# One-hot matrices built after the residual split, and gates applied one expert step earlier, in a two-block transformer kernel

## The reference, cut to what matters

```
g = jax.nn.softmax(best, axis=-1)
u = expert_u[idx]
act = jax.nn.gelu(jnp.einsum('td,thkd->thk', xc, u), approximate=False)
w = (g * act).astype(h.dtype)
return jnp.einsum('thk,thkd->td', w, expert_v[idx])
```

## Time and profile before

| | us |
|---|---|
| median of 3 runs | 1471.93 |
| the 3 runs | 1464.92, 1471.93, 1472.66 |
| the profiled execution, its own time | 1464.92 |
| its span, first to last instruction | 1463.6 |
| PE busy | 1386.9 (95%) |
| DVE busy | 980.6 (67%) |
| ACT busy | 638.5 (44%) |

### The profile page before, as it was taken

The page is one execution under the profiler, slowest core; times in us unless marked ns, Lnnn a source line. Parts: engine busy times, 40 slices in busy tenths (PEclk is TensorE's granted clock), DMA queues, the critical chain, the costliest instruction groups (busy, mean ns, idle before and its releaser), DMA issues.

```text
span 1463.6 us, 22358 instructions
## 1 busy us (share of the span) xinstructions
PE 1386.9 (95%) x9318; PEld 966.8 (66%) x9318; DVE 980.6 (67%) x1555; ACT 638.5 (44%) x851; POOL 153.7 (10%) x138
## 2 busy tenths in 40 slices
PE   6999899899999798959999999999999999999998
PEld 5655798478864355535888889999997444444443
DVE  2433786389984666557658998899997555555555
ACT  2341422166753433444525454544444444444443
POOL 0221523124530000000010300000000000000000
PEclk9999999899999999979999999999999999999999
DMA  6312000285664342233606655555446565565651
GB/s 259 144 60 84 1 2 1 89 298 180 213 225 144 136 180 72 102 115 116 230 30 235 225 182 197 174 173 180 168 170 229 199 204 202 202 244 201 202 202 57
DMA packets 33140, 231.50 MB, mean 158 GB/s; under 512 B 3712, under 2 KB 3984, under 8 KB 6160
## 3 DMA queue, kind: packets, MB, share of 16 engines
q1 hardware_dynamic: 31968, 227.02, 43.9%
q10 hardware_dynamic: 720, 1.73, 0.3%
q0 software_dynamic: 352, 1.32, 0.2%
HBM read 227.96 MB, written 2.10 MB: 157 GB/s over the span
## 4 chain that ended last, share of the span: by engine, by line
PE 87%; DVE 5%; ACT 4%; issue 3%; DMA 0%; POOL 0%; ACTq 0%; DVEq 0%; POOLq 0%
PE bank L583 21%; PE bank L589 21%; PE bank L586 21%; PE bank L606 7%; PE bank L1191 2%; PE bank L674 2%; PE bank L902 2%; PE bank L733 2%; PE bank L1155 1%; DVE arena L1299 1%; PE bank L691 1%; PE bank L873 1%; PE bank L799 1%; ACT arena L2220 1%; PE bank L790 1%
## 5 line engine op out<-in xcount | busy, mean ns | idle before, releaser
L583 PE MATMUL bank<-arena 128*128 128x256 f16 (+3 forms) x600 | 186.7, 313 | 11.1 <-DVE arena L1291 5.8
L586 PE MATMUL bank<-arena 128*128 128x256 f16 (+3 forms) x600 | 186.5, 313 | 0.0
L589 PE MATMUL bank<-arena 128*128 128x256 f16 (+3 forms) x600 | 186.5, 313 | 0.0
L1299 DVE SCALAR_TENSOR_TENSOR arena<-ring,arena 128x2048 f16<-128x2048 f32 (+1 forms) x59 | 133.7, 2273 | 46.2 <-ACT arena L2220 46.0
L2220 ACT ACTIVATE arena<-ring 128x2048 f16<-128x2048 f32 (+1 forms) x59 | 111.0, 1892 | 37.9 <-PE bank L589 37.9
L2041 DVE SCALAR_TENSOR_TENSOR HT<-ring,HT 128x2048 f16<-128x2048 f32 x41 | 93.9, 2290 | 40.9 <-ACT HT L2581 40.7
L2610 ACT CAST cst<-arena 128x512 f16<-128x512 f32 x64 | 39.4, 617 | 174.2 <-PE bank L589 171.2
L2041 DVE SCALAR_TENSOR_TENSOR ring<-ring 128x2048 f16<-128x2048 f32 x42 | 96.1, 2289 | 28.1 <-ACT ring L2581 27.8
L2041 DVE SCALAR_TENSOR_TENSOR X<-ring,X 128x2048 f16<-128x2048 f32 x42 | 96.1, 2289 | 26.1 <-ACT X L2581 26.0
L1191 PE MATMUL bank<-ring,arena 128*128 128x128 f16 x512 | 98.6, 219 | 0.0
L583 PE MATMUL bank<-cst,X 128*128 128x256 f16 x336 | 91.5, 272 | 0.0
(11 more groups left out here) (355 smaller groups left out, 3323.6 us busy)
## 6 DMA issues: line engine op xcount, KB each, us to landing
ring<-in_expert_u SPq DMA_DIRECT2D x64, 1024.0 KB, 4.9
ring<-in_expert_v SPq DMA_DIRECT2D x64, 1024.0 KB, 4.8
ring<-in_w_in_n SPq DMA_DIRECT2D x24, 1024.0 KB, 4.9
ring<-in_w_up_t SPq DMA_DIRECT2D x22, 1024.0 KB, 5.3
ring<-in_w_down_n SPq DMA_DIRECT2D x11, 1024.0 KB, 4.9
ring<-in_w_out_n SPq DMA_DIRECT2D x8, 1024.0 KB, 4.8
ring<-in_w_query_t SPq DMA_DIRECT2D x8, 1024.0 KB, 5.0
ring<-in_w_in_t SPq DMA_DIRECT2D x3, 1024.0 KB, 7.1
```

The costliest lines, as they stand in the source:

```text
L583: pe.matmul(out_, stat[0], mov[0], start=start, stop=False)
L586: pe.matmul(out_, stat[0], mov[1], start=False, stop=False)
L589: return pe.matmul(out_, stat[1], mov[0], start=False, stop=stop)
L1299: nv.scalar_tensor_tensor(out=lo, in0=ld.slot(i), scalar=W_UP, in1=hi, op0=ALU.mult, op1=ALU.subtract).then_inc(s["split_lo"], 1)
```

## The change: what it does

```
-GATES_IN = {LATE + 35 * g // 31: g for g in range(32)}
+GATES_IN = {LATE + 36 * g // 31: g for g in range(32)}
...
     for q in range(WHOLE, 64):
+        expert_lo(q + 2 - WHOLE)
+        for _ in range(SEARCH.get(q, 0)):
+            next(chosen)
         if q == SLOTS_AFTER[1] + 1:
             next(slots_evicted(1))
         if q + 1 in GATES_IN:
             one_hots(GATES_IN[q + 1])
-        expert_lo(q + 2 - WHOLE)
-        for _ in range(SEARCH.get(q, 0)):
-            next(chosen)
-        if q - 1 in GATES_IN:
-            weigh(GATES_IN[q - 1])
-        if q > LATE:
-            weigh_late(q - 1)
-    w_lo(0)
-    w_lo(1)
-    weigh_late(63)
+        if q in GATES_IN:
+            weigh(GATES_IN[q])
+        if q == 63:
+            w_lo(0)
+            w_lo(1)
+        if q >= LATE:
+            weigh_late(q)
...
-        expert_hi(q + 3 - WHOLE)
         if q in GATES_IN:
             keep_gates(GATES_IN[q])
+        expert_hi(q + 3 - WHOLE)
```

## The result

The changed kernel takes 1478.61 us (median of 9 runs, 1477.68 to 1487.11) against 1464.92 (9 runs, 1463.48 to 1472.66; the first three of these are the ones shown above). The medians are 13.7 us apart, 0.93%. The ratio on record, into which 26 runs of the changed kernel went, is 1.0105, with a 95% interval of 1.0084 to 1.0127: slower by about 1%. The prediction was +13.6 us on the profiled execution, and 1485.5 as the median.

The account below looks back on a forecast made before the run. PE alone was taken to bound the stage, each new wait paid in full. Stalls of 14.8 us less 1.2 at the end gave +13.6: 1478.5 us profiled, median 1485.5, range 1474 to 1489.

Parts of the forecast that it names:

- The one-hots behind the residual: Steps 26 to 62: chain of 8.32 us early, 7.84 late, makes PE's gate matmuls wait; 14.8 us of stalls together.
- The two-step rule: Two PE steps last at least 13.05 us early, 12.57 late, so among neighbours with gates every second step stalls.
- The copies ahead of `expert_hi`: ACT's gate copies lengthen the chain to the one-hots by 0.65 us early, 0.17 late; no row shows them there.
- The weighing one step earlier: On DVE, ahead of the residual, ending near 2.2 us early, 2.9 late: costs nothing early, about nothing late.
- The end of the stage: PE's start of the second stage loses 0.61 us instead of 1.80, a gain of 1.2 us.
- The table: PE's work stays the same; a fifth step without gates adds one dearer stall, already included; expert_v's later load costs nothing.
- The sum and the median: Whole kernel: +13.6 us, profiled execution 1478.5 us, median 1485.5 us.
- the choice of level: Forecast median set at 1471.93 + 13.6, the level where two of the three runs shown stood.
- A: Rival: one-hots come in time for the gate matmuls, only the end's 1.2 us gain remains; 1470.7 us, chance 0.09.
- B: Rival: early chain 0.5 us shorter, neighbours' stalls nearly go, six large ones remain; +5 us, 1477, chance 0.07.
- C: Rival: stalls make PE's clock fall, 3.4 us each; six falls give 1506 us, two 1492; chance 0.08.
- D: Rival: DVE is the bound throughout; expected to bind in the last third alone, so counted within the forecast.

Follow-up runs that it names:

- e1: The changed kernel with the one-hots first again, ahead of the residual; ratio 0.9996 to the kernel before, stage -1.0 us.
- e2: The kernel before with only the one-hots moved behind the residual; ratio 1.0054, stage +8.1 us.
- e5: The kernel before with the one-hots behind the residual and the gate copies ahead of expert_hi; ratio 1.0118, stage +13.9 us.
- e6: The kernel before with only the gate copies moved ahead of expert_hi; ratio 1.0008, stage 0.0 us.
- e7: The changed kernel with the gate copies behind expert_hi again; ratio 1.0296 to the kernel before, stage +40.9 us.
- e10: The changed kernel with the one-hots ahead of the residual and the copies behind expert_hi again; ratio 1.004 to the kernel before, stage +5.0 us.
- e9: The kernel before with the new table alone, groups spread to step 62; ratio 1.0019, stage +1.4 us.
- e4: The changed kernel with PE's gate matmuls begun after the first expert matmul of a step instead of 13; ratio 1.0258 to the kernel before, stage +37.7 us.
- the first four experiments: The runs e1 to e4, beside which runs of the kernel before were taken.
- e8: The changed kernel with the one-hots first again and w_lo(0), w_lo(1) ahead of the last residual; ratio 0.9973 to the kernel before, stage -1.8 us.
- e3: The changed kernel with PE's gate matmuls begun after 25 expert matmuls instead of 13; ratio 0.9989 to the kernel before, stage +0.2 us.

## Why the prediction was right

**The one-hots behind the residual.** Right in mechanism and size. The chain measured 8.28 us against 8.32. By groups of steps the losses were 3.5, 2.7, 2.5, 2.4, 2.9 and 1.3 us (26 to 32, 34 to 38, 41 to 45, 48 to 53, 55 to 60, 62) against 3.6, 2.8, 2.5, 2.2, 2.55 and 1.18: 15.4 in all against 14.8. That the place of the one-hots is the cause is shown from both sides: restored alone, the loss is gone (e1), made alone, it is 8.1 us (e2), and with the copies 13.9 (e5).

**The two-step rule.** Right for the first three groups. In the last two it was only nearly so. The losses there are 1.27, 0.33, 0.40, 0.43, 0.46 us in steps 55 and 57 to 60, step after step and not every second one: DVE's pass of 6.56 us is the bound there, as the prediction had it for steps 55 to 60 with +0.6 us (its own numbers give 0.5). It began one group earlier, from step 51 (0.19, 0.22, 0.25), where DVE after already has nothing idle and a pass is longer than PE's 6.15:

```profile
1057.48 1.05 DVE L2067 SCALAR_TENSOR_TENSOR arena<-bank,arena 128x400 f32<-128x400 f32 x2
1063.84 1.07 DVE L2067 SCALAR_TENSOR_TENSOR arena<-bank,arena 128x408 f32<-128x408 f32 x2
```

That is 6.36 us, 0.21 over PE's step. The prediction looked at the longest passes alone.

**The copies ahead of `expert_hi`.** The unknown of the sum, taken as 0.65 us, was 0.61. Their cost of about 6 us exists only together with the late one-hots (e5, e6).

**The weighing one step earlier.** Costs nothing where the one-hots lead (e1), and nothing early. Late it was to cost "about nothing", and that is 0.2 us at the stage's last residual. That it depends on the copies being first was not in the prediction; e7 and e10 show it.

**The end of the stage.** Forecast 0.61 us lost instead of 1.80; measured 0.77 by the starts (0.60 of recorded idle). The 0.16 more is the weighing ahead of the last residual. The gain is 1.0 us (e1), not 1.2.

**The table.** Taken by itself, it costs 1.4 us at the end of the stage in the old order (e9). The prediction never asked this, since in the new order the last group is weighed in time. That the fifth step without gates adds one of the dear stalls fits the 1.30 us at step 62; no run has the new order with the old table.

**The sum and the median.** In the stage the sum was 0.7 us too small: +14.3 against +13.6, most of it in the stalls and 0.2 at the end. That the profiled execution came out at 1478.06, so close to the forecast 1478.5, is in part luck: it was 1.2 us ahead before the stage began. The point forecast of 1485.5 was 7 us too high, since I set it on the level of two of the three runs shown, and with six more runs the median of the kernel before was 1464.92. The step at fault is the choice of level. Which level a median of nine falls on is chance too: in later groups of 29, 23 and 19 runs the kernel before had medians of 1466.59, 1466.57 and 1466.51. The range held both.

**The rivals.** A (in time) is refuted by 18 recorded waits. B is what e2 looks like: the large stalls remain and the others nearly go. C did not happen in the changed kernel: 1.00 with waits up to 1.38 us. It did happen in e7 and, once, in e4, so it was no idle rival. In this stage no run had a fall after a wait under 2.40 us. Its price was twice too high: the prediction took 3.4 us for a fall, and in e7 one cost 1.7. The rule of the Trainium skill that it drew on ("TensorE: Matmul & The Clock Gate", section "A second HAM failure mode: psum-queue depth-cycling") speaks of idles that are short and frequent; those of the changed kernel, 0.2 to 1.4 us every 6.5 to 19 us, did not swing the clock. The falls in e4 and e7 came after waits of 2.40 us and more. D held in the last third only.

## What to carry to other kernels

When the bounding engine takes its work in order, give each operand that another engine makes a deadline, and write down by how much it is met; a reordering that costs no work can eat that room, and beyond it every tenth of a microsecond is paid at each second step. An edit that is free alone (e6) can cost 6 us with another, and undoing one that seems to cost can make things worse (e7), so such an order is to be tested by its pairs. Where one engine serves two consumers from one queue, the product that waits for nothing (the one-hots) goes ahead of the one that waits for the longest chain (the residual).

## What the runs showed of the hardware that was not expected

The spread of the times, most near 1464 and 1472 us for the kernel before, goes with PE's clock, and it does not arise in this stage. Of 29 runs of it, taken beside the first four experiments, the 12 with a mean granted clock of 0.977 or more took 1462.96 to 1464.91, the 12 with 0.971 or less 1471.81 to 1475.46, and the 5 between (0.974 to 0.976) 1466.55 to 1466.78. So there are levels in between, and not two alone. The profiled executions of e8 and e3 are of the low clock, and show where. From 240 to 270 us, where its program is that of the kernel before, first before, then e8:

```profile
240.00:270.00 30.00, 23.17 (x152) 19.89 (x152) 18.40 (x35) 4.84 (x9) 7.75 (x5) 0.81 0.22 82
```

```profile
240.00:270.00 30.00, 28.56 (x143) 26.26 (x142) 13.84 (x27) 4.85 (x9) 6.54 (x5) 0.60 0.00 1
```

The granted clock of this stretch is lower (0.60 against 0.81; 0.58 in e3), and fewer matmuls get through it while PE is busy for longer. Matmul by matmul, e8 is 0.2 us behind the kernel before at 239 us and 8.2 behind at 290; it comes to step 24's end at 898.26 us where the kernel before comes at 890.48. What decides it from run to run, no run here shows. For a change of 1% it means that three runs are too few to know the median's level, and that a distance inside the profile, as used above, tells a microsecond where the whole time does not.

A wait of 2.4 to 3.0 us may or may not be followed by the lower clock: it was after 2.59, 2.76, 2.93 and 2.40 us in e7 and after one of 2.51 in e4, and it was not after 2.41 to 2.69 (five times) in e4, 2.40 in e10 and 3.03 in e9. One fall cost 1.7 us, at the second stage's start and within the stage alike.
